# A two-layer encoder trunk on one core: layer 1 transposes its residual once for two norms, and some casts, copies and small loads change places

## The reference

```python
def rmsnorm(x, g):
    return x * rsqrt(mean(x * x, axis=-1) + EPS) * g

kd, vs = split(rmsnorm(x, kv_norm_g) @ w_kv_shared)        # end of layer 0
h = rmsnorm(x, mix_norm_g[1])                              # start of layer 1
qd, qm = split(h @ w_q_b)
q1, q2 = rotary(qd[..., 0]), rotary(qd[..., 1])            # keys likewise
a = softmax(q1 @ k1 * scale) - lam * softmax(q2 @ k2 * scale)
o = rmsnorm(a @ vs, subln_g) * (1 - lam_init)
y_mem = softmax(qm @ mk * scale) @ mv
x = x + concat(o, y_mem) @ w_out[1]
```

## Time and profile before

| | |
|---|---|
| median of 3 runs | 1425.39 us (1425.25 to 1425.84) |
| profiled execution | 1424.84 us |
| its span, first to last instruction | 1423.1 us |
| PE busy | 1405.4 us, 99% |
| DVE busy | 1144.0 us, 80% |
| ACT busy | 953.2 us, 67% |
| POOL busy | 51.9 us, 4% |
| granted PE clock | 0.998 of full speed |
| read from HBM | 433.36 MB, 309 GB/s over the span |

### The profile page before, as it was taken

The page is one execution under the profiler, slowest core; times in us unless marked ns, Lnnn a source line. Parts: engine busy times, 40 slices in busy tenths (PEclk is TensorE's granted clock), DMA queues, the critical chain, the costliest instruction groups (busy, mean ns, idle before and its releaser), DMA issues.

```text
span 1423.1 us, 20481 instructions
## 1 busy us (share of the span) xinstructions
PE 1405.4 (99%) x7646; PEld 1199.2 (84%) x7646; DVE 1144.0 (80%) x1032; ACT 953.2 (67%) x878; POOL 51.9 (4%) x81
## 2 busy tenths in 40 slices
PE   8999999999999999999999999999999999999997
PEld 8988999998988888888888888888888888888885
DVE  6686544447786999888888888888889898888997
ACT  6556433346466777777777777777777777777775
POOL 2100000002001000000000000000000000000100
PEclk9999999999999999999999999999999999999999
DMA  9753655554526999999999999999999999999993
GB/s 316 247 171 121 205 186 195 181 178 159 182 90 255 376 379 377 372 387 380 379 373 377 382 371 379 390 370 378 377 383 381 376 376 377 377 393 357 323 369 122
DMA packets 207564, 439.95 MB, mean 309 GB/s; under 512 B 7309, under 2 KB 54433, under 8 KB 207506
## 3 DMA queue, kind: packets, MB, share of 16 engines
q1 hardware_dynamic: 202912, 423.65, 82.1%
q0 software_dynamic: 4576, 15.51, 3.1%
q10 hardware_dynamic: 18, 0.01, 0.0%
HBM read 433.36 MB, written 5.78 MB: 309 GB/s over the span
## 4 chain that ended last, share of the span: by engine, by line
PE 93%; DVE 3%; ACT 1%; DMA 1%; POOL 0%; SPq 0%; issue 0%; ACTq 0%; DVEq 0%
PE bank L1966 29%; PE bank L1968 29%; PE bank L1967 29%; PE bank L2669 2%; DMA raw<-in_w_in_a_dram 1%; DVE wlo L1156 1%; PE bank L2179 1%; ACT whi L714 1%; PE bank L2576 0%; PE bank L2229 0%; PE bank L2210 0%; PE bank L2070 0%; DVE hn L1190 0%; PE bank L2564 0%; PE bank L1981 0%
## 5 line engine op out<-in xcount | busy, mean ns | idle before, releaser
L1156 DVE TENSOR_TENSOR wlo<-raw,whi 128x2048 fp32r<-128x2048 f32 x396 | 903.4, 2290 | 177.4 <-ACT whi L714 175.9
L714 ACT CAST whi<-raw 128x2048 fp32r<-128x2048 f32 x396 | 756.2, 1914 | 201.9 <-PE bank L1968 195.7
L1966 PE MATMUL bank<-whi,op_hi 128*128 128x512 f32 (+1 forms) x1160 | 438.0, 378 | 2.4 <-DVE op_lo L1548 1.5
L1968 PE MATMUL bank<-whi,op_lo 128*128 128x512 f32 (+1 forms) x1160 | 430.2, 371 | 0.0
L1967 PE MATMUL bank<-wlo,op_hi 128*128 128x512 f32 (+1 forms) x1160 | 429.7, 370 | 0.0
L1966 PEld LDWEIGHTS bank<-whi,op_hi 128*128 128x128 f32 x1160 | 218.6, 188 | 44.0 <-DVE wlo L1156 4.2
L1968 PEld LDWEIGHTS bank<-whi,op_lo 128*128 128x128 f32 x1160 | 218.5, 188 | 38.2
L1967 PEld LDWEIGHTS bank<-wlo,op_hi 128*128 128x128 f32 x1160 | 218.7, 189 | 35.3
L1966 PE MATMUL bank<-whi,h2T_hi 128*128 128x512 f32 x544 | 213.9, 393 | 1.0 <-DVE h2T_lo L1597 0.6
L1968 PE MATMUL bank<-whi,h2T_lo 128*128 128x512 f32 x544 | 211.9, 390 | 0.0
L1967 PE MATMUL bank<-wlo,h2T_hi 128*128 128x512 f32 x544 | 211.9, 389 | 0.0
(11 more groups left out here) (343 smaller groups left out, 805.4 us busy)
## 6 DMA issues: line engine op xcount, KB each, us to landing
raw<-in_w_gate_up_moe_dram SPq DMA_DIRECT2D x223, 1024.0 KB, 7.3
raw<-in_w_down_moe_dram SPq DMA_DIRECT2D x109, 1024.0 KB, 7.4
raw<-in_w_gate_up_dense_dram SPq DMA_DIRECT2D x22, 1024.0 KB, 5.1
raw<-in_w_down_dense_dram SPq DMA_DIRECT2D x11, 1024.0 KB, 5.0
raw<-in_w_in_a_dram SPq DMA_DIRECT2D x10, 1024.0 KB, 12.2
raw<-in_w_out_dram SPq DMA_DIRECT2D x8, 1024.0 KB, 4.9
raw<-in_w_kv_shared_dram SPq DMA_DIRECT2D x6, 1024.0 KB, 5.1
raw<-in_w_q_b_dram SPq DMA_DIRECT2D x4, 1024.0 KB, 5.3
```

What stands on the lines that cost most here:

```text
L714: a.copy(whi[:, c % SPLIT, :], src).then_inc(hi_ready, 1)
L1156: d.tensor_tensor(wlo[:, c % SPLIT, :], src, whi[:, c % SPLIT, :].bitcast(F32), ALU.subtract).then_inc(lo_ready, 1)
L1966: m.matmul(dst, sh, mh, start=start and i == 0, stop=False)
L1968: last = m.matmul(dst, sl, mh, start=False, stop=stop and i == n - 1)
```

## The change

1. **The start.** small_w and b_f get a semaphore of their own, forget_in, and POOL waits for raw_in[5] before the other six. small_hi and small_lo go ahead of the cast and the split of unit 3. `mem_rows` goes ahead of `project_mem_queries` and into bank 7.
2. **Layer 0.** copy0(8) is called ahead of the casts of its turn.
3. **The dense SwiGLU.** On ACT the cast of D goes ahead of silu, the last h2_hi ahead of the cast of U_KV; on DVE two residual additions go ahead of the split of U_KV.
4. **The norm.** PE transposes X itself, once. The gains (head_g, one column per chunk) are multiplied in by ACT and DVE when they fill the operands: for K and V chunk by chunk and tile by tile (128x128), for the queries once for both tiles (128x256). The row factor is multiplied in when the products leave PSUM (`take`), for the memory queries in the max and as the scale of the exponential. The multiplies of POOL and DVE with whole gain rows, ACT's scaling of tile 1 and two loads of gain rows go. The second unit is now vd 0 and the third qd 0.
5. **The heads of layer 1.** The split of U_KV+7 moves from turn 1 into turn 2, that of U_MOE-1 from turn 8 behind the last head_norm, and the load of the root table behind copy and squares of turn 8.

```diff
-        + [("kd", 0), ("qd", 0), ("vd", 0), ("qm", 1)]
+        + [("kd", 0), ("vd", 0), ("qd", 0), ("qm", 1)]
...
-    return 4 + (p - P_M1 if p < P_KV else (p - P_KV) % 3)
+    if p < P_KV:
+        return 4 + p - P_M1
+    return p - P_KV if p < P_KV + 4 else 4 + (p - P_KV) % 3
...
             pool.wait_ge(raw_in[1], 16)
+            with nc.allow_non_contiguous_dma("small columns"):
+                for dst, src in firsts:
+                    pool.dma_start(dst, src).then_inc(forget_in, 16)
+            pool.wait_ge(raw_in[5], 16)
...
+                for i, g1 in enumerate((kv_norm_g, mix_norm_g[1])):
+                    pool.dma_start(head_g[:, i, :], g1.rearrange("(k p) -> p k", p=P)).then_inc(router_in, 16)
...
             norm_fill_hi(1)
+            act.wait_ge(forget_in, 16 * N_FIRST)
+            a.copy(small_hi[:], small_w[:]).then_inc(small_hi_ready, 1)
             split_until(4)
-            act.wait_ge(small_in, 16 * N_SMALL)
-            a.copy(small_hi[:], small_w[:]).then_inc(small_hi_ready, 1)
...
+                    if s == 8:
+                        copy0(s)
                     for u in ended_in(s):
                         split_until(u + 4)
-                    copy0(s)
+                    if s != 8:
+                        copy0(s)
...
+                    row = stat[:, 4, 3, t:t + 1] if SETS1[g][0] == "mem" else 1.0
                     ins = a.activation(pr[:, c0:c1], b[:, c0:c1], ACT.Exp, bias=negm[:, S1 + g, t:t + 1],
-                                       accum_out=rsum[:, S1 + g, t:t + 1])
+                                       scale=row, accum_out=rsum[:, S1 + g, t:t + 1])
...
+            def kv_fill_hi(t):
+
+                for c in range(KC):
+                    act.wait_ge(tr_ready, 16 + 4 * t + c // 2 + 1)
+                    c0 = SEQ * (c % 2) + P * t
+                    ins = a.activation(op_hi[KV_BUF][:, c, P * t:P * (t + 1)], bank[4 + c // 2][:, c0:c0 + P], ACT.Copy,
+                                       scale=head_g[:, 0, c:c + 1])
+                    if c % 2:
+                        ins.then_inc(fill_hi, 1)
+
+            def mix_fill_hi():
+
+                for c in range(KC):
+                    act.wait_ge(fill_lo, int(FILL[4]) + 4 + c // 2 + 1)
+                    c0 = SEQ * (c % 2)
+                    ins = a.activation(op_hi[MIX_BUF][:, c, :], bank[4 + c // 2][:, c0:c0 + SEQ], ACT.Copy,
+                                       scale=head_g[:, 1, c:c + 1])
...
                     split_hi(U_FFN + ffn_pos("U", j), it)
+                    split_hi(U_FFN + ffn_pos("D", j - 1), it)
                     ffn_silu(j, it)
-                    split_hi(U_FFN + ffn_pos("D", j - 1), it)
                     split_hi(U_FFN + ffn_pos("G", j + 1), it)
+            ffn_h2_hi(FFN_STEPS - 1)
             split_hi(U_KV)
-            ffn_h2_hi(FFN_STEPS - 1)
...
-            norm_sqrt(4, 0)
+            act.wait_ge(router_in, 64)
+            kv_fill_hi(0)
             split_hi(U_KV + 1)
-            tile_fill_hi(4, 0)
-            sum_squares(2, x_added, 0)
-            sum_squares(3, x_added, 0)
-            tile_fill_hi(5, 0)
-            norm_sqrt(4, 1)
...
+            for q in range(2, 4):
+                sum_squares(q, x_added, 0)
+            kv_fill_hi(1)
+            for t in range(NT):
+                norm_sqrt(4, t)
+            mix_fill_hi()
...
+                if SETS1[g][0] == "mem":
+                    step(ins)
+                    ins = d.tensor_tensor(negm[:, S1 + g, :], negm[:, S1 + g, :], stat[:, 4, 3, :], ALU.mult)
...
             def mem_rows():
 
                 pe.wait_ge(mem_scale_ready, 1)
+                pe.wait_ge(hn_ready, 4)
...
+            def tile_transposes(t):
+
+                pe.wait_ge(x_added, 2 * t + 2)
+                if t:
+                    pe.wait_ge(fill_lo, int(FILL[4]) + 4)
+                for c in range(KC):
+                    c0 = SEQ * (c % 2) + P * t
+                    last = m.transpose(bank[4 + c // 2][:, c0:c0 + P], X[:, t, P * c:P * (c + 1)], ident[:])
...
+            pe.wait_ge(fill_lo, int(FILL[4]) + 4)
             project(18, (0,))
-            pe.wait_ge(fill_lo, int(FILL[4]) + 4)
+            tile_transposes(1)
             project(19, (0,))
-            tile_transposes(4, 1)
-            tile_transposes(5, 1)
...
+            pe.wait_ge(fill_lo, int(FILL[4]) + 8)
+            project(18, (1,))
+            project(19, (1,))
+            pe.wait_ge(fill_lo, int(FILL[5]))
             project(20)
```

More of the change, by code:

```diff
@@ L225 @@
 S1, R1 = N0, N0
-N_SMALL = 8
+N_FIRST, N_SMALL = 2, 6
 LOGIT_COPIES = 12
@@ L649, in _ @@
                    allow_small_or_imprecise_dtypes=True).then_inc(slots_ready, 1)
[L650 to L653, removed]
+            load_gain(6, 12)
             pool.wait_ge(gain_in, 16 * 2)
-            for n, dst, g1 in ((4, hn, gain[:]), (5, tok, mix_gain)):
-                for h in range(2):
-                    cols = slice(512 * h, 512 * (h + 1))
-                    pool.wait_ge(x_added, 3 + h)
-                    g.tensor_tensor(dst[:, 1, cols], X[:, 1, cols], g1[:, cols], ALU.mult).then_inc(kv_gained, 1)
-            pool.wait_ge(kv_gained, 4)
-            load_gain(6, 18)
-            pool.wait_ge(gain_in, 16 * 3)
             for t in range(NT):
@@ L912, in applied_act @@
                     mem_pair_hi(h // 2)
-            def tile_fill_hi(n, t):
-                for h in range(2):
-                    act.wait_ge(tr_ready, 16 + 4 * t + 2 * (n - 4) + h + 1)
-                    a.copy(op_hi[FILL_BUF1[n - 4]][:, 4 * h:4 * h + 4, t * P:(t + 1) * P],
-                           bank[TR_BANK1[n - 4][t] + h][:].rearrange("p (c n) -> p c n", c=4)).then_inc(fill_hi, 1)
+            def kv_fill_hi(t):
[12 more added lines that the diff above has]
+                                       scale=head_g[:, 1, c:c + 1])
+                    if c % 2:
+                        ins.then_inc(fill_hi, 1)
             def ffn_silu(j, turns=0):
@@ L1609, in _ @@
             ffn_h2_lo(FFN_STEPS - 1)
-            split_lo(U_KV)
             add_tile(0)
             add_tile(1)
+            split_lo(U_KV)
             norm_mean(4, 0, 2)
-            norm_scale(4, 0)
-            for n in (4, 5):
-                for h in range(2):
-                    apply_gain(n, X, 4, 0, h)
+            kv_fill_lo(0)
             add_tile(2)
-            tile_fill_lo(4, 0)
             add_tile(3)
             split_lo(U_KV + 1)
-            tile_fill_lo(5, 0)
             norm_mean(4, 1, 2)
-            kv_scale()
-            tile_fill_lo(4, 1)
-            tile_fill_lo(5, 1)
+            kv_fill_lo(1)
+            head_scales()
+            mix_fill_lo()
             split_lo(U_KV + 2)
@@ L1672, in _ @@
                     split_lo(U_KV + 6)
-                if c == 1 and 0 < i < 9:
+                if i == 2:
+                    split_lo(U_KV + 7)
+                if c == 1 and 0 < i < 8:
                     split_lo(unit_of(p) + 3)
@@ L2001, in mem_rows @@
                 pe.wait_ge(mem_scale_ready, 1)
+                pe.wait_ge(hn_ready, 4)
                 for t in range(NT):
-                    last = m.matmul(bank[0][:, P * t:P * (t + 1)], stat[:, 0, 3, t:t + 1].to_broadcast([P, P]),
+                    last = m.matmul(bank[7][:, P * t:P * (t + 1)], stat[:, 0, 3, t:t + 1].to_broadcast([P, P]),
                                     ident[:], start=t == 0, stop=t == NT - 1)
@@ L2072, in one_pass @@
                     return last
+                mem_rows()
                 pe.wait_ge(hi_ready, 3)
@@ L2403, in ffn_up, with ffn_down @@
                 last.then_inc(unit_used, 1)
-            def ffn_down(j, it=0, moved=0, first=False, final=False, parts=(0, 1), between=None):
+            def ffn_down(j, it=0, moved=0, first=False, final=False, parts=(0, 1)):
                 c = U_FFN + ffn_pos("D", j)
@@ L2421, in ffn_down @@
                             last.then_inc(acc_ready, 1)
-                        if between is not None and t == 1 and h == 0:
-                            between()
                 if 1 in parts:
```

122 lines of the change are left out of this document (58 added, 64 removed).

## The result

The changed kernel takes **1433.54 us** (median of 5, 1432.60 to 1433.79) where before takes 1425.39 (median of 5, 1425.06 to 1425.84): ratio 1.0052, interval 1.0041 to 1.0063. By the medians it is 8.15 us slower, by the ratio 7.4 us, where 5.0 us less was forecast.

A forecast was written before the change was run, and what follows sets the result against it. PE was taken as the bound, busy 99% of the span; gains 2.2 + 2.2 + 0.6 = 5.0 us off 1424.84 gave 1419.8, plus 0.55 for the median 1420.4; range 1418.2 to 1422.3.

The forecast's parts named there:

- Nothing that the change touches runs there: Experts: PE alone is busy, 819.98 of 820.00 us, and the change touches nothing there, so gains come only elsewhere.
- The slower rival: PSUM fills: ACT and DVE take turns on a bank, adding 6.1 us, giving 1426.5; chance 0.04.
- The sign that was to give the alarm: Experts: PE should stay busy 820 of 820 us; if not, the whole sum is wrong.
- A, 2.2: Start: mem_rows fills a PE gap and the wait for small_lo goes; gain 2.2 us, bounds 1.0 to 2.3.
- B, 2.2 out of 4.3 with a new wait of 2.2: Norm ahead of layer 1: 4.3 us saved, about 2.2 lost to a new wlo wait at project(20); gain 2.2.
- 11.95 - 9.65: Norm, from the second transposes: ACT and DVE chain to U_KV+2's split, 11.95 us, less PE's work, 9.65.
- all gaps named: Norm: PE's gap of 0.56 us at 326.64 and waits of 0.83 and 0.69 for op_lo would go.
- The bounds: Norm: gain between 4.3 us (no new wait) and about 0 (small instructions as long as single ones).
- C, 0.6: Heads of layer 1: about 0.3 us from the prob wait and 0.3 from tok; 0.6, from -0.5 to 1.3.
- the second rival: Layer 1's first softmax: scale pointers and a multiply delay probabilities 0.4 to 0.5 us, giving 1421.5; chance 0.20.
- What stays: Heads of layer 1: PE's wait of 0.8 us for op_lo stays; the 0.7 for probT stays as well.

The follow-up runs named there:

- A alone: The kernel before with only the start's edits (forget loads first, small_hi earlier, mem_rows in bank 7), no tile moved: 1424.07 us, ratio 0.9984.
- the second profile: The changed kernel, unaltered, profiled and timed once more: median 1432.90 us, ratio 1.0049; its profiled run took 1430.81 us.
- the first profile: The changed kernel's original profiled run, against the kernel before: 1433.79 us, where before's profiled run took 1424.84 us.

## Why the prediction was wrong, point by point

**The step that failed** is the first one: "Nothing that the change touches runs there", said of the experts. The edits of the engines' programs don't, but head_g moved h2T by 64 bytes, and the experts' down products took 5 to 6 ns more each. The pair before and before with 64 bytes, which differ in nothing but this padding, put its price at 10.5 us. No rival had it. The slower rival was of another kind (turns on PSUM banks, for which the fills would have had to be longer than they were, below), and its sign was right by accident. The sign that was to give the alarm was blind: "The experts should keep 820 of 820; if they do not, the whole sum is wrong". They kept 819.97 of 820 at a clock of 1.00, and the sum was wrong all the same. Busy time says that PE never stood still, not how fast its matmuls ran; the count in the same stretch, 3695 for 3730, would have said it.

**The sum itself** can be read where the tiles are unmoved, from how far the change with head_g last is ahead of before at the same instruction (profiled 1420.56 against 1424.84, so 4.3 in all; 4.4 by the ratio, forecast 5.0).

- *A, 2.2:* 1.83 ahead at the transposes near 97.6 (99.47 before); 2.23 in the repeat of the changed kernel, 2.3 by A alone. Right. In the profile with 1.83 the cast ahead of the memory fill had waited for its weight load until 19.60 (19.03 before), and PE still waited 0.67 for op_hi behind mem_rows. mem_rows stands in the gap, small_lo was ready at 28.34 in the changed kernel, and unit 3's split was not late.
- *B, 2.2 out of 4.3 with a new wait of 2.2:* PE comes to project(20) at 347.48 where it came at 352.01: 4.53, so B gave 2.7. The wait is there and takes 1.81. The prediction's own numbers give 11.95 - 9.65 = 2.3 for it and 4.3 - 2.3 = 2.0 for B, where it wrote 2.2 both times. The chain was 0.5 shorter than counted: 11.48 in the changed kernel, from the transposes at 338.31 to the end of the wait at 349.79, in which PE had 9.67 of work. Its terms: eight 128x128 of ACT 2.3 as forecast, 2.18 measured; eight 128x256 3.2, measured 3.08; all gaps named are gone. The bounds were right, and the choice between them was 0.5 too low. From the trace after:

```profile
L922 ACT ACTIVATE op_hi<-bank,head_g 128x128 fp32r<-128x128 f32 x16 | 4.4, 384 | 2.9 <-PE bank L2351 2.9
...
L932 ACT ACTIVATE op_hi<-bank,head_g 128x256 fp32r<-128x256 f32 x8 | 3.1, 554 | 0.0
```

- *C, 0.6:* gave -0.2 (4.35 ahead at the last output product). The wait of 0.56 for prob fell to 0.35 for probT, 0.2 won where 0.3 was counted. But about 0.2 went at each of two places, ahead of the first probabilities' transposes (367.16, 4.27 ahead) and at the scores near 385.7 (0.15 for prob). This is the second rival, "the first softmax gets late", in small. And tok kept its whole 0.5, of which 0.3 was to go: ACT's squares had to wait 0.41 for the copy, the load of the root table behind them ended at 426.43, and the root at 426.54 is 4.34 ahead of before's 430.88, no more than PE is. The exps with a second pointer:

```profile
L870 ACT ACTIVATE prob<-bank,negm 128x256 f32<-128x256 f32 x12 | 5.7, 472 | 4.6 <-DVE negm L1485 4.6
...
L870 ACT ACTIVATE prob<-bank,negm,stat 128x256 f32<-128x256 f32 x8 | 4.4, 560 | 11.2 <-DVE negm L1488 11.2
```

The pointer costs 88 ns, where I had taken 0.1 and then counted nothing, since "ACT had room behind it". The Trainium skill, ScalarE: Activation LUTs, section "What ACT_TABLE_LOAD costs", has about 93 ns for each pointer operand: the trace agrees, with 88 for the second. That these 88 ns and the multiply of negm make the two losses of 0.2 was not tried by a run of its own.
- *What stays:* probT kept 0.8, op_lo 0.8, as forecast.

With everything in its place: -2.2 - 2.7 + 0.2 = -4.7 by parts (-4.3 in the one profile), and +10.5 for the address, gives 1431, which is what the second profile took; the measured median of 1433.5 has falls of the clock on top, 3.0 for both in the first profile. They were not in the forecast either. The first fall is in many runs of before too; the second, 1.6 of the 3.0, would make it 1432.8, an estimate, and the last 0.7 is open.

## What to carry to other kernels

Read a diff for its tiles as well as for its instructions: a new small tile in the middle of the SBUF declarations moves all that are declared after it. Declare small tiles last, or pad them to 256 bytes; here that was worth 10.5 us, more than twice the whole change. The same place modulo 256 is not best for every form: the 128x256 products gained 3.6 us away from it. When the same instructions get some nanoseconds longer at full clock with no wait, compare the groups by shape and ask what the slow ones read; compare the count of matmuls in a stretch too, for busy time hides it. And ahead of each weight cast on a busy ScalarE, see whether a table load or a square root that nobody waits for yet stands in its way: moving them took away a wait of 1.8 us.

## What the runs showed of the hardware that I had not expected

- A matmul of 128x512 takes 390 ns with its stationary and moving operands at the same address modulo 256 bytes, 395 with 64 or 128 between them, 390 to 392 with 192. One of 128x256 is slowest at 0 (283) and takes 277 to 279 at 64 and 192. Moving all tiles together changes nothing. The weight loads of the 128x512 products keep 188 ns; those of the 128x256 products take 192 at 0 and 188 at 64 and 192. Why is open; offsets under 64 bytes were not tried.
- These few ns are real time where PE bounds: 10.5 us lost, 3.7 won, by unused bytes alone.
- TensorE's granted clock can fall for some us behind a wait of 1.8 us in one execution (0.50 between 352 and 354) and stay at 1.00 behind the same wait in another. At the start it fell in 7 of 17 profiles, in the start of before and in that of the change.
